# A two-layer hybrid backbone on one core: the place of two transposes and of one low part in the first layer's norms

## The chip, the cores and the metric

The kernel runs on one core of a Trainium2 chip. The metric is the device time of one execution in microseconds (us), lower is better; a figure for a kernel is the median of its runs.

## The reference

Two layers over 512 latent and 256 context tokens of width 1024, in float32. What matters here is where the norms stand:

```python
for layer in range(DEPTH):                    # DEPTH = 2
    y_l, y_c = mixer(modulate(x, sh1, sc1), modulate(ctx, csh1, csc1), w_in[layer], ...)
    x = post_norm(x, g1 * y_l, ln1_w, ln1_b)  # layer_norm(ALPHA * x + g1 * y_l) * w + b
    x = post_norm(x, g2 * swiglu(modulate(x, sh2, sc2), w_gate_up, w_down), ln2_w, ln2_b)
    # in the first layer the same for ctx
# modulate(x, shift, scale) = layer_norm(x) * (1 + scale) + shift
```

So after the mixer's output projection every token goes through a post-norm with weight and bias, and then through a second, plain norm with a modulation, before the next weight product can read it. The same stands after the feed-forward part, where the next product is the next layer's input projection.

## The kernel before

The 768 tokens lie as six tiles of 128 tokens (`tiles`; the first layer uses all six, `nt = 6`). A weight product keeps float32 accuracy by splitting both operands into a high and a low part of a reduced format: one product (`product`, lines 822 to 824) is three matmuls. GpSimd splits the weights as they come (line 736 the high part, line 739 the low one) into a ring of eight slots, and TensorE frees a slot by raising `ring_used` in its work on the last tile. For the activations ScalarE writes the high part (`high`, line 1626, into `act_hi`) and VectorE the low part (`low_part`, line 2122, into `act_lo`). Each engine has its own program with the order of its work written out; semaphores join them.

The last pass of a projection ahead of a norm (`last_pass`) goes tile by tile, eight products each (index `j`, 0 to 7). As soon as a tile's sum is complete, the norm of that tile begins on the other engines, so that the norms run beside the products of the later tiles. For the tile with number n in a norm the steps are:

- VectorE takes the sum out of PSUM (lines 2131 and 2133 or 2135), makes statistics (2150, 2153), and applies the post-norm in `affine` (2204, 2206, 2211; the last one also sums the row). Lines 2204 and 2211 are the long steps, of 128x1024 elements.
- ScalarE takes the square root for the first norm (1589), then squares for the second norm (1596, `sd2`, which waits for line 2211) and takes its root (1599).
- VectorE turns it into a scale (`second_scale`, 2217 and 2218).
- ScalarE writes the normed tile to `xn` (1607, `normalize`).
- TensorE transposes it, eight 128x128 pieces into PSUM banks 6 and 7 (`transposes`, 918).
- ScalarE modulates it into `hbuf` (1613; for the last two tiles VectorE does half of it, 2183) and writes the high part (1626), and VectorE the low part (2122).

VectorE's and ScalarE's loops (`norm_steps` in each program) are skewed by steps. In VectorE's, step s has, in this order: `affine(s - 1)`, `low_part(s - 3)`, `modulate_half(s - 2)` (which does something for the last two tiles alone), the sum and statistics of tile s, `second_scale(s - 1)`. In ScalarE's, step s has `normalize(s - 2)`, `sd2(s - 1)`, `modulate(s - 2)`, the first root of tile s, `high(s - 2)`.

TensorE's transposes stand at fixed places in its own order. Tiles 0, 1 and 2 are transposed within the last pass, in its fourth, fifth and sixth tile, behind the product `j` that `NORM_SPOT` gives for that norm. A key is (layer, norm): (0, 1) is the first layer's norm after the mixer, (0, 2) the one after the feed-forward. Tiles 3, 4 and 5 are transposed in the work that follows. After norm (0, 1) that is the first gate-and-up chunks (`part` in `gate_up`): six parts of 48 matmuls with 256 columns, two chunks for each pair of tiles, the first chunk with weights in buffers of their own (`own_hi`, `own_lo`), the second from the ring. The transposes of tiles 3, 4 and 5 stand behind the first three parts, and the third and the fifth part wait for the low part of the pair's second tile (`wait_low`). After norm (0, 2) it is the next layer's input projection, eight products per tile, and transposes of tiles 3, 4 and 5 stand behind its first three tiles.

GpSimd splits the second gate-and-up unit as ring slots come free, and waits before the third for the low part of tile 4 (`wait_low(pool, ...)`). The norm (1, 1) (`MID`) has an order and places for its transposes of its own.

Of the kernel before, what the change touches and what calls it, by code (L numbers as in the profile page):

```python
# [41 lines left out]
SEGMENTS = {"win": [4] * 9, "modB": [0] * 8, "modG": [0] * 4, "wout": [4] * 4,  # L42
            "gu0": [4] * HALF, "dn0": [4, 4, 3, 3, 4, 4], "gu1": [4] * HALF, "dn1": [4, 4, 3, 4, 4, 3]}
KEPT = (3, 8)
NORM_SPOT = {(0, 1): (4, 5, 7), (0, 2): (3, 5, 6), (1, 1): (1,)}
MOD_BLOCKS = {"modA": [0, 1, 2, 3], "modB": [6, 7, 8, 9], "modG": [4, 5], "modC": [10, 11]}
START_TILES = [2, 3, 0, 4, 1, 5]

# [96 lines left out]
def build(nc, x, c, ctx_in, c_ctx, w_mod, b_mod, w_in, a_q_norm, a_k_norm, b_sink, f_mix, r_decay,  # L145
# [3 lines left out]
    with stack:  # L149
# [409 lines left out]
        def low_count(key, n):  # L559

            return n + 1 + (n + 1) // 2 if key == MID else n + 1
# [42 lines left out]
        def need(e, name, l, n):  # L604

            before = NORMS[:NORMS.index(l)] if isinstance(l, tuple) else range(l)
            e.wait_ge(sem(name), n + sum(signals(name, k) for k in before))
# [211 lines left out]
        def _(pe):  # L819
# [89 lines left out]
            def transposes(key, n):  # L909

                need(pe, "xn_ready", key, n + 1)
                if n > 0:
                    need(pe, "h_ready", key, n)
                    if shared_modulation(key, n - 1):
                        nt = len(tiles_of(key[0]))
                        need(pe, "h_half", key, signals("h_half", key) - (nt - n))
                for k in range(KC):
                    mm = nc.tensor.transpose(ps[:, 6 + k // 4, (k % 4) * P:(k % 4 + 1) * P], xn[:, n % 2, k * P:(k + 1) * P],  # L918
                                             ident[:, :])
                mm.then_inc(sem("xn_T"), 1)  # L920
# [445 lines left out]
            def last_pass(l, key, tiles, seg, p, g, m, left, ready):  # L1366

                nt = len(tiles)
                for n, t in enumerate(tiles):
# [3 lines left out]
                    for j in range(8):  # L1373
# [23 lines left out]
                        if key == MID:  # L1397
                            if (n, j) in ((2, 5), (3, 7)):
                                transposes(key, n - 2)
                        elif n >= 3 and key != (DEPTH - 1, 2) and j == NORM_SPOT[key][n - 3]:  # L1400
                            transposes(key, n - 3)
# [700 lines left out]
        def _(dve):  # L2102
# [3 lines left out]
            def link(ins):  # L2106

                step_no[0] += 1
                ins.then_inc(sem("dve_step"), 1)
                dve.wait_ge(sem("dve_step"), step_no[0])  # L2110
# [3 lines left out]
            def done(ins, name):  # L2114

                raised[name] = raised.get(name, 0) + 1
                ins.then_inc(sem(name), 1)
                dve.wait_ge(sem(name), raised[name])

            def low(dst, src, high):  # L2120

                return v.tensor_tensor(dst, src, high.bitcast(F32), ALU.subtract)
# [15 lines left out]
            def tail_part(h):  # L2138

                if h == 0:  # L2140
                    need(dve, "dn_acc", DEPTH - 1, 4 * (len(LAT) - 1) + 1)
                else:
                    dve.wait_ge(ring_used, dn_slot(DEPTH - 1, 3, HALF - 1) + 1)
                cols = slice(512 + h * 256, 768 + h * 256)
                link(v.tensor_tensor(tail_acc(h), tail_acc(h), bc[:, 0, cols], ALU.mult))  # L2145
                link(v.tensor_tensor(X[:, TAIL, cols], X[:, TAIL, cols], tail_acc(h), ALU.add))  # L2146
                link(v.bn_stats(st[:, TAIL, 6 + 6 * h:12 + 6 * h], X[:, TAIL, cols]))  # L2147

            def half_stats(t, o, h):
                return v.bn_stats(st[:, t, o + 6 * h:o + 6 * h + 6], X[:, t, h * 512:(h + 1) * 512])  # L2150

            def variance(t, o, signal):
                done(v.bn_aggr(st[:, t, o + 12:o + 14], st[:, t, o:o + 12]), signal)

            def norm_steps(key, tiles, first):
# [6 lines left out]
                def low_part(n):  # L2162
                    if not last and 0 <= n < len(tiles):
                        need(dve, "h_hi", key, low_count(key, n))
                        c = slice(tiles[n] * P, (tiles[n] + 1) * P)
                        done(low(act_lo[:, :, c], hbuf[:, n % 2, :].rearrange("p (k t) -> p k t", k=KC), act_hi[:, :, c]), "low_ready")
# [8 lines left out]
                def modulate_half(n):  # L2175
                    if last or not 0 <= n < len(tiles) or not shared_modulation(key, n):
                        return
                    need(dve, "xn_T", key, n + 1)
                    if n >= 2:
                        wait_low(dve, key, n - 2)  # L2180
                    stream = 0 if tiles[n] >= CT else 1
                    for k in range(4):
                        ins = v.tensor_scalar(hbuf[:, n % 2, k * P:(k + 1) * P], ps[:, 6, k * P:(k + 1) * P],  # L2183
                                              mod_col[:, 2 * which + 1, k, stream:stream + 1],
                                              mod_col[:, 2 * which, k, stream:stream + 1], ALU.mult, ALU.add)
                    done(ins, "h_half")

                def affine(n):
                    t = tiles[n]
                    if last and t == TAIL:  # L2190
                        halves = [slice(h * 512, (h + 1) * 512) for h in range(2)]
                        for c in halves:
                            ins = v.scalar_tensor_tensor(X[:, t, c], X[:, t, c], st[:, t, 18:19], bc[:, 2, c],  # L2193
                                                         ALU.subtract, ALU.mult)
                        link(ins)
                        need(dve, "sd1", key, n + 1)
                        link(v.reciprocal(st[:, t, 21:22], st[:, t, 20:21]))
                        for c in halves:
                            v.scalar_tensor_tensor(X[:, t, c], X[:, t, c], st[:, t, 21:22], bc[:, 3, c],  # L2199
                                                   ALU.mult, ALU.add).then_inc(sem("x_ready"), 1)  # L2200
                        return
                    if n == 0:
                        need(dve, "norm_in", key[0], 32 * key[1])
                    link(v.scalar_tensor_tensor(X[:, t, :], X[:, t, :], st[:, t, 12:13], bc[:, 2, :], ALU.subtract, ALU.mult))  # L2204
                    need(dve, "sd1", key, n + 1)
                    link(v.reciprocal(st[:, t, 15:16], st[:, t, 14:15]))
                    if last:
                        done(v.scalar_tensor_tensor(X[:, t, :], X[:, t, :], st[:, t, 15:16], bc[:, 3, :],  # L2208
                                                    ALU.mult, ALU.add), "x_ready")
                        return  # L2210
                    done(v.scalar_tensor_tensor(X[:, t, :], X[:, t, :], st[:, t, 15:16], bc[:, 3, :],
                                                ALU.mult, ALU.add, accum_out=st[:, t, 17:18]), "sum2")

                def second_scale(n):
                    t = tiles[n]
                    need(dve, "sd2", key, n + 1)
                    link(v.reciprocal(st[:, t, 32:33], st[:, t, 31:32]))
                    done(v.scalar_tensor_tensor(st[:, t, 33:34], st[:, t, 17:18], -1.0 / D, st[:, t, 32:33],
                                                ALU.mult, ALU.mult), "scale2")

                nt = len(tiles)
# [6 lines left out]
                if key == MID:  # L2228
# [23 lines left out]
                    low_half(3, 1)  # L2252
                    return
                for step in range(nt + 3):
                    if 0 < step <= nt:
                        affine(step - 1)
                    low_part(step - 3)
                    modulate_half(step - 2)
                    if last and step == nt - 1:
                        for h in range(2):  # L2260
                            tail_part(h)
                        done(v.bn_aggr(st[:, TAIL, 18:20], st[:, TAIL, 0:18]), "var1")
                    elif step < nt:
                        first(step, tiles[step])
                        link(half_stats(tiles[step], 0, 1))
                        variance(tiles[step], 0, "var1")
                    if 0 < step <= nt and not last:
                        second_scale(step - 1)
# [421 lines left out]
            for l in range(DEPTH):  # L2690
                tiles = tiles_of(l)
                nt = len(tiles)
# [53 lines left out]
```

## Time and profile before

| what | value |
| --- | --- |
| median of 3 runs | 1644.21 us (1642.68 to 1645.06) |
| profiled execution | 1643.62 us |
| its span, first to last instruction | 1641.8 us |
| TensorE matmuls busy | 1593.6 us, 97% |
| GpSimd busy | 855.9 us, 52% |
| VectorE busy | 778.2 us, 47% |
| ScalarE busy | 427.9 us, 26% |
| granted TensorE clock, mean | 0.998 of full speed |

The busy shares are means over stages of different kinds. The two norms of the change are short stages, 380 to 434 us and 950 to 1000 us, in which VectorE and ScalarE are nearly as busy as TensorE. Times in the rows are counted from the span's start. Matmuls are pipelined: a row's duration overlaps the next row's, so the pace of TensorE is read from the starts.

### The profile page before, as it was taken

The numbers are of one execution on the slowest core, as the hardware profiler recorded it, in microseconds if no ns is written. First come the engines' busy times: TensorE is split into PE (matmuls) and PEld (weight loads), VectorE is DVE, ScalarE is ACT, GpSimd is POOL, SyncE is SP. The second block draws the span as 40 slices with busy tenths as digits, with TensorE's granted clock in tenths as the row PEclk, the third lists the DMA queues.
The fourth block names the chain that finished last, engine by engine and source line by source line (L and its number), as shares of the span: only waits on it lengthen the run. The fifth ranks groups of instructions, "written<-read, shape, count | busy, mean of one in ns | idle before, by whom it ended". The sixth has DMA issues, their size and how long they took to land. (4 is left out here: it accounts for less than half of the span.)

```text
span 1641.8 us, 23300 instructions
## 1 busy us (share of the span) xinstructions
PE 1593.6 (97%) x9341; PEld 1359.3 (83%) x9341; DVE 778.2 (47%) x1200; ACT 427.9 (26%) x919; POOL 855.9 (52%) x850
## 2 busy tenths in 40 slices
PE   7999999999999999999999999999999999999997
PEld 5788766778999988899999888876777888888886
DVE  4462265549663414544554396715658322420038
ACT  5512365425400011100002064216534200200011
POOL 4643133643564444544445546613484777777772
PEclk9999999999999999999999999999999999999999
DMA  9312143121353312243652122210032642233321
GB/s 344 113 52 78 47 141 118 54 80 52 118 165 91 116 39 77 82 137 116 194 191 79 46 77 69 78 34 9 15 89 69 188 145 75 93 102 103 103 90 52
DMA packets 161369, 160.89 MB, mean 98 GB/s; under 512 B 6520, under 2 KB 120296, under 8 KB 161264
## 3 DMA queue, kind: packets, MB, share of 16 engines
q1 hardware_dynamic: 140928, 121.40, 24.4%
q10 hardware_dynamic: 20336, 38.03, 7.1%
q8 instruction: 74, 1.21, 0.3%
q14 instruction: 31, 0.25, 0.1%
HBM read 157.31 MB, written 2.10 MB: 97 GB/s over the span
## 5 line engine op out<-in xcount | busy, mean ns | idle before, releaser
L736 POOL TENSOR_SCALAR ring_hi<-stage 128x512 fp32r<-128x512 f32 x352 | 247.1, 702 | 523.9 <-PE ps L824 446.4
L739 POOL TENSOR_TENSOR ring_lo<-stage,ring_hi 128x512 fp32r<-128x512 f32 x352 | 480.6, 1365 | 29.4
L822 PE MATMUL ps<-act_hi,ring_hi 128*128 128x384 f32 (+2 forms) x1088 | 379.4, 349 | 2.1 <-POOL ring_lo L739 2.1
L824 PE MATMUL ps<-act_hi,ring_lo 128*128 128x384 f32 (+2 forms) x1088 | 377.8, 347 | 0.0
L823 PE MATMUL ps<-act_lo,ring_hi 128*128 128x384 f32 (+2 forms) x1088 | 377.8, 347 | 0.0
L822 PE MATMUL ps<-ring_hi,act_hi 128*128 128x512 f32 (+1 forms) x711 | 280.7, 395 | 1.9 <-ACT gate_ret L1755 1.5
L824 PE MATMUL ps<-ring_hi,act_lo 128*128 128x512 f32 (+1 forms) x711 | 273.5, 385 | 0.0
L823 PE MATMUL ps<-ring_lo,act_hi 128*128 128x512 f32 (+1 forms) x711 | 273.1, 384 | 0.0
L822 PEld LDWEIGHTS ps<-act_hi,ring_hi 128*128 128x128 f32 x1088 | 204.6, 188 | 15.9 <-POOL ring_lo L739 2.7
L823 PEld LDWEIGHTS ps<-act_lo,ring_hi 128*128 128x128 f32 x1088 | 204.6, 188 | 13.1
L824 PEld LDWEIGHTS ps<-act_hi,ring_lo 128*128 128x128 f32 x1088 | 204.5, 188 | 13.1
L2592 DVE TENSOR_TENSOR hid<-silu_g,ps 128x768 f32<-128x768 f32 (+1 forms) x44 | 36.1, 821 | 302.5 <-ACT silu_g L1981 302.2
L1981 ACT ACTIVATE silu_g<-ps 128x768 f32<-128x768 f32 (+1 forms) x44 | 31.0, 706 | 556.8 <-PE ps L824 526.8
L822 PEld LDWEIGHTS ps<-ring_hi,act_hi 128*128 128x128 f32 x711 | 133.7, 188 | 33.3 <-issue 6.4
L824 PEld LDWEIGHTS ps<-ring_hi,act_lo 128*128 128x128 f32 x711 | 133.6, 188 | 27.2
L823 PEld LDWEIGHTS ps<-ring_lo,act_hi 128*128 128x128 f32 x711 | 133.8, 188 | 26.2 <-issue 1.4
L749 POOL TENSOR_SCALAR probs<-probs,rden 128x768 f32<-128x768 f32 (+3 forms) x50 | 38.0, 767 | 133.7 <-DVE rden L2394 133.7
L2407 DVE SCALAR_TENSOR_TENSOR mod_acc_ffn<-mod_stage,c_silu,mod_acc_ffn 128x512 f32<-128x512 f32 x84 | 78.9, 966 | 16.7 <-DMA mod_stage<-in_w_mod_dram 14.9
L822 PE MATMUL ps<-ring_hi,hs_hi 128*128 128x512 f32 x220 | 86.6, 394 | 0.1
L824 PE MATMUL ps<-ring_hi,hs_lo 128*128 128x512 f32 x220 | 85.6, 389 | 0.0
L823 PE MATMUL ps<-ring_lo,hs_hi 128*128 128x512 f32 x220 | 85.6, 389 | 0.0
L2386 DVE TENSOR_REDUCE negmax<-ps 128x1 f32<-128x768 f32 (+4 forms) x80 | 57.8, 763 | 56.7 <-PE ps L1057 36.9
(278 smaller groups left out, 2040.2 us busy)
## 6 DMA issues: line engine op xcount, KB each, us to landing
stage<-in_w_gate_up_dram SPq DMA_DIRECT2D x88, 512.0 KB, 5.1
mod_stage<-in_w_mod_dram ACTq DMA_DIRECT2D x56, 512.0 KB, 4.1
stage<-in_w_in_dram SPq DMA_DIRECT2D x18, 1024.0 KB, 5.0
stage<-in_w_down_dram SPq DMA_DIRECT2D x16, 1024.0 KB, 5.0
stage<-in_w_mod_dram SPq DMA_DIRECT2D x12, 1024.0 KB, 5.2
start_mod<-in_w_mod_dram SPq DMA_DIRECT2D x16, 512.0 KB, 9.7
stage<-in_w_down_dram SPq DMA_DIRECT2D x8, 768.0 KB, 4.4
stage<-in_w_out_dram SPq DMA_DIRECT2D x16, 256.0 KB, 4.5
```

What stands on the lines that cost most here:

```text
L736: nc.gpsimd.tensor_scalar(hi_, stage[:, par, j * 512:(j + 1) * 512], 1.0, 0.0, ALU.mult, ALU.add).then_inc(w_hi, 1)
L739: nc.gpsimd.tensor_tensor(lo_, stage[:, par, j * 512:(j + 1) * 512], hi_.bitcast(F32), ALU.subtract).then_inc(w_ready, 1)
L749: nc.gpsimd.tensor_scalar(probs_slot(2 * i + a)[:, 0:n], probs_slot(2 * i + a)[:, 0:n], rden[:, m:m + 1], 0.0, ALU.mult, ALU.add).then_inc ...
L822: nc.tensor.matmul(o, a_hi, b_hi, start=first, stop=False)
L823: nc.tensor.matmul(o, a_hi, b_lo, start=False, stop=False)
L824: return nc.tensor.matmul(o, a_lo, b_hi, start=False, stop=last)
L1981: ins = a.activation(silu_g[:, e, lo_col:TOK].rearrange("p (r n) -> p r n", r=parts if fh or f > 1 else len(tiles_of(l)) // 2), gate_acc(l ...
L2386: v.tensor_reduce(negmax[:, m:m + 1], flat[:, 0:n], AX, ALU.max, negate=True).then_inc(sem("neg_ready"), 1)
L2407: return v.scalar_tensor_tensor(acc, w, c_k, acc, ALU.mult, ALU.add)
L2592: done(v.tensor_tensor(hid[:, j, lo_col:TOK].rearrange("p (r n) -> p r n", **pat), silu_g[:, e, lo_col:TOK].rearrange("p (r n) -> p r n", ...
```

## The change

Three edits. In norm (0, 1) the transposes of tile 1 stand behind product 7 of the fifth tile in place of product 5. In norm (0, 2) they stand behind product 6 in place of 5. In norm (0, 1), in VectorE's step 6 (`step == nt`), the low part of tile 3 stands ahead of `affine(5)` in place of behind it. The entry for (1, 1) is dropped from the table.

```diff
--- before.py
+++ after.py
@@ -42,7 +42,7 @@
 SEGMENTS = {"win": [4] * 9, "modB": [0] * 8, "modG": [0] * 4, "wout": [4] * 4,
             "gu0": [4] * HALF, "dn0": [4, 4, 3, 3, 4, 4], "gu1": [4] * HALF, "dn1": [4, 4, 3, 4, 4, 3]}
 KEPT = (3, 8)
-NORM_SPOT = {(0, 1): (4, 5, 7), (0, 2): (3, 5, 6), (1, 1): (1,)}
+NORM_SPOT = {(0, 1): (4, 7, 7), (0, 2): (3, 6, 6)}
 MOD_BLOCKS = {"modA": [0, 1, 2, 3], "modB": [6, 7, 8, 9], "modG": [4, 5], "modC": [10, 11]}
 START_TILES = [2, 3, 0, 4, 1, 5]
 
@@ -2252,9 +2252,12 @@
                     low_half(3, 1)
                     return
                 for step in range(nt + 3):
+                    if step == nt and key == (0, 1):
+                        low_part(step - 3)
                     if 0 < step <= nt:
                         affine(step - 1)
-                    low_part(step - 3)
+                    if step != nt or key != (0, 1):
+                        low_part(step - 3)
                     modulate_half(step - 2)
                     if last and step == nt - 1:
                         for h in range(2):
```

## Rows read from the trace of the kernel before

**Rows 1.** Stretches: us; busy us of PE, PEld, DVE, ACT, POOL; clock; DMA share, GB/s

```profile
434.00:959.00 525.00, 525.00 (x2857) 494.20 (x2856) 246.06 (x275) 51.41 (x66) 266.49 (x255) 1.00 0.37 114
```

**Rows 2.** Timeline of TensorE, first norm: start, duration, instruction, idle before and its releaser

```profile
396.85 0.39 PE L823 MATMUL ps<-ring_lo,act_hi 128*128 128x512 f32 x1
397.07 0.39 PE L824 MATMUL ps<-ring_hi,act_lo 128*128 128x512 f32 x1
398.29 1.09 PE L918 MATMUL ps<-ident_r,xn 128*128 128x128 f32 x8 [0.83 <-ACT xn L1607]
399.14 0.48 PE L822 MATMUL ps<-ring_hi,act_hi 128*128 128x512 f32 x1
...
420.01 1.09 PE L918 MATMUL ps<-ident_r,xn 128*128 128x128 f32 x8
421.90 0.39 PE L822 MATMUL ps<-act_hi,own_hi 128*128 128x256 f32 x1 [0.79 <-DVE act_lo L2122]
...
427.76 1.03 PE L918 MATMUL ps<-ident_r,xn 128*128 128x128 f32 x8
428.55 0.36 PE L822 MATMUL ps<-act_hi,ring_hi 128*128 128x256 f32 x1
```

**Rows 3.** Timeline of ScalarE, first norm

```profile
413.34 1.15 ACT L1596 ACTIVATE xn<-resid,st 128x1024 f32<-128x1024 f32 x1 [1.05 <-DVE resid L2211]
...
417.75 1.09 ACT L1626 ACTIVATE act_hi<-hbuf 128x1024 fp32r<-128x1024 f32 x1
418.70 1.26 ACT L1607 ACTIVATE xn<-resid,st 128x1024 f32<-128x1024 f32 x1
420.62 1.15 ACT L1596 ACTIVATE xn<-resid,st 128x1024 f32<-128x1024 f32 x1 [0.66 <-DVE resid L2211]
...
424.58 1.23 ACT L1607 ACTIVATE xn<-resid,st 128x1024 f32<-128x1024 f32 x1
```

**Rows 4.** Timeline of VectorE, first norm

```profile
403.46 1.28 DVE L2211 SCALAR_TENSOR_TENSOR resid<-resid,st,bc 128x1024 f32<-128x1024 f32 x1
404.78 1.51 DVE L2122 TENSOR_TENSOR act_lo<-hbuf,act_hi 128x1024 fp32r<-128x1024 f32 x1
...
409.02 0.40 DVE L2218 SCALAR_TENSOR_TENSOR st<-st 128x1 f32<-128x1 f32 x1
409.45 1.60 DVE L2204 SCALAR_TENSOR_TENSOR resid<-resid,st,bc 128x1024 f32<-128x1024 f32 x1
...
411.29 2.01 DVE L2211 SCALAR_TENSOR_TENSOR resid<-resid,st,bc 128x1024 f32<-128x1024 f32 x1
...
417.77 1.29 DVE L2204 SCALAR_TENSOR_TENSOR resid<-resid,st,bc 128x1024 f32<-128x1024 f32 x1
...
420.62 1.22 DVE L2122 TENSOR_TENSOR act_lo<-hbuf,act_hi 128x1024 fp32r<-128x1024 f32 x1
```

**Rows 5.** Timeline of GpSimd, first norm

```profile
404.34 0.88 POOL L736 TENSOR_SCALAR ring_hi<-stage 128x512 fp32r<-128x512 f32 x1 [23.66 <-PE ps L824]
405.31 2.12 POOL L739 TENSOR_TENSOR ring_lo<-stage,ring_hi 128x512 fp32r<-128x512 f32 x1
...
408.10 1.30 POOL L739 TENSOR_TENSOR ring_lo<-stage,ring_hi 128x512 fp32r<-128x512 f32 x1
...
410.07 2.15 POOL L739 TENSOR_TENSOR ring_lo<-stage,ring_hi 128x512 fp32r<-128x512 f32 x1
...
426.15 0.62 POOL L736 TENSOR_SCALAR ring_hi<-stage 128x512 fp32r<-128x512 f32 x1 [10.15 <-issue]
```

**Rows 6.** Timelines of TensorE and ScalarE, second norm

```profile
967.58 1.09 PE L918 MATMUL ps<-ident_r,xn 128*128 128x128 f32 x8 [0.66 <-ACT xn L1607]
...
988.03 1.05 PE L918 MATMUL ps<-ident_r,xn 128*128 128x128 f32 x8
...
981.07 1.15 ACT L1596 ACTIVATE xn<-resid,st 128x1024 f32<-128x1024 f32 x1 [0.15 <-DVE resid L2211]
...
986.67 1.26 ACT L1607 ACTIVATE xn<-resid,st 128x1024 f32<-128x1024 f32 x1
```

## The prediction

> **What bounds the kernel now.** I read the page's engine table first: TensorE is the engine that is hardly ever idle, so time is won or lost where it stands still, or where it is held for other engines. The table of stretches then says where not to look: from 434 to 959 us TensorE is busy 525.00 of 525.00 us [rows 1]. What it is late by at 434 it is late by at 959. Both places that the change touches are at the two ends of that stretch: the first layer's first norm (380 to 434 us) and its second (950 to 1000 us). Call the six transposes of a norm T0 to T5, one per tile in order of work.
>
> In the first norm the timeline of TensorE shows two stalls [rows 2]. Before T1 it issued matmuls at 396.85 and 397.07, could have gone on at 397.30, and started T1 at 398.29, released by ScalarE's xn: 0.99 us lost. Before the part for the third and fourth tiles it waited for VectorE's low part, at 421.90. The timelines of ScalarE [rows 3], VectorE [rows 4] and GpSimd [rows 5] show what stands behind them: ScalarE's and VectorE's steps are written out in one order, so an instruction that waits holds everything behind it.
>
> **T1 two products later, first norm.** A product is three matmuls; six matmuls at this pace of just under 0.23 us are 1.36 us, so T1 is reached at 398.66, after xn (398.25). No wait is left. A T that waited cost 0.85 us to the next matmul (398.29 to 399.14), one that didn't 0.79 (427.76 to 428.55) [rows 2]. So TensorE is ahead by 0.99 + 0.06 = 1.05 us. How far? T4 started at 420.01, 0.05 after ScalarE's xn for it (418.70 + 1.26 = 419.96) [rows 2, 3]. ScalarE's xn is fed from VectorE: its square pass started at 413.34, as VectorE's long step from 411.29 for 2.01 us ended [rows 3, 4]. Nothing in this chain waits for T1. T4 therefore doesn't move, and by itself the 1.05 us is worth 0 at T4.
>
> But one thing does start earlier: GpSimd. Its first split started at 404.34 when TensorE's work on the last tile had freed a ring slot [rows 5]. Now that is at 403.29. At 403.46 VectorE starts an affine step of 1.28 us (L2211) [rows 4]. Before, VectorE was first, and GpSimd's split took 0.88 instead of 0.62. Rows where GpSimd was first: the low part at 404.78 took 1.51 instead of 1.22 (GpSimd's L736 ended 405.22); L2211 at 411.29 took 2.01 instead of 1.28 (L739 from 410.07 ended 412.22); the small step at 409.02 took 0.40 and ended with L739, at 409.40 [rows 4, 5]. The other way, L739 at 405.31 took 2.12 instead of 1.30 and ended 1.14 after the low part's end at 406.29. So whoever comes second waits for the first's end. In the sum I use these distances: a long VectorE step ends 1.07 after GpSimd's end, L739 1.15 after VectorE's end, L736 0.48 after.
>
> Replayed with GpSimd at 403.29: L736 ends 403.91. VectorE's L2211 (403.46) is held, +0.30, ends 405.04. L739 ends 406.19. The low part (405.08) is held by it, ends 407.26: +0.96. L736 ends 407.74, L739 409.12, L736 409.71; the next L739 starts 409.78 and ends 411.08, just ahead of VectorE's small step, now at 409.99: +0.95. L2204 at 411.13 is held by the last L736 (ends 411.67): +0.33. L2211 at 412.98 is held by the last L739 (ends 413.89): +0.70, ends 414.96. That is 3.24 us of holding where before there were 0.29 + 0.24 + 0.31 + 0.73 = 1.57: VectorE's step for the fifth tile ends 1.67 us later. Ends for this term: 0 if GpSimd comes after 403.46 (0.17 us of margin decides, and then the pattern of before repeats); 0.6 if the small step at 409.99 slips ahead of L739 (margin 0.21); 1.8 if all are held longest. I take 1.67, nearest to the rows.
>
> The Trainium skill, page "SBUF — State Buffer", section "Who interferes with whom", states this as a rule: VectorE instructions with two SBUF inputs and GpSimd instructions that read SBUF take a shared port as an exclusive lock, and whoever issues first holds it for its whole length. The trace agrees, with the pairs above. By a rule of shared bandwidth both would be slowed in proportion, whatever the order, and the term would be near 0.
>
> **The fourth tile's low part first, first norm.** Before: affine(5) at 417.77, the low part at 420.62, 1.22 us [rows 4]. The low part needs ScalarE's high part, from 417.75 [rows 3], done 418.84 (1.09 long). With about 0.1 for the hand-over (estimate; ScalarE to TensorE took 0.05 above) it runs from 418.95 to 420.17. TensorE's wait at 421.90 is gone: T4 at 420.01 plus 0.85 lets it go on at 420.86, so 1.04 us is won here. Ends for it: 0 and 1.04.
>
> What is queued behind the waiting low part is affine(5): from 420.20 instead of 417.77, +2.43. ScalarE's square pass for the last tile (420.62) waits for that, and behind it stand, in ScalarE's order, the fifth tile's modulation and high part and the last tile's xn at 424.58 [rows 3]. All go 2.43 later. That xn was done at 425.81, and T5 at 427.76 didn't wait: 1.95 us of cover [rows 2, 3]. Now it is done at 428.24, T5 starts 428.29 and the next matmul 429.14 instead of 428.55: +0.59, where TensorE alone would have been 1.04 early. So the won wait comes back, larger, at T5. GpSimd's unit at 426.15 [rows 5] waits for the fifth low part and moves by as much, but TensorE asks for its slots only after two more parts of 5.8 us, and no wait follows.
>
> Both parts together: the 1.67 shifts the whole chain from 413.34 on. xn of T4 comes at 421.63 (TensorE is there a good 2 us before), and T5's next matmul at 429.14 + 1.67 = 430.81 against 428.55: **+2.26 us** at 434, kept to 959. VectorE's own steps between (low part of the third tile ends 416.2) are done before the later high part, so they add nothing. The last low part still has about a us before the third pair's part asks for it.
>
> **T1 one product later, second norm.** T1 waits there, at 967.58 [rows 6], by 0.82 (0.66 idle, plus the tail of the matmul before); one product is 0.68, so it still waits 0.14, starts when it did, and the 0.68 is taken out behind it. Again T4 bounds it: TensorE reached it at 988.03, while xn was ready at 987.93. ScalarE needed 5.60 us from square pass to xn (981.07 to 986.67), in the first norm for the same steps 5.36 (413.34 to 418.70), since T3 held it a little [rows 3, 6]. That 0.24 goes; with it T4 comes at 987.74, 0.29 earlier, and costs 0.06 more as one that waits: **-0.23 us**. Ends: 0 and -0.68. GpSimd stands still in this stage. The dropped table entry (1, 1) is read by nobody: that norm's spots stand in code of their own. No DMA is moved in its queue; stage loads only follow GpSimd.
>
> **Sum.** +2.26 - 0.23 = +2.03 us on the profiled execution's 1643.62 (span 1641.8 and 1.8 around it) is 1645.65. It stands 0.59 below the median of the runs, 1644.21; on that, 1646.2.
>
> **The rivals.**
> *No collision (25%).* GpSimd's earlier start doesn't hold VectorE more than before. For it: 0.17 us decides, and GpSimd's records are the roughest. Against: a short lead was enough before (L2204 at 409.45 took 1.60, held by a split that can't have started until the L739 of 408.10 was over, at 409.40). Then +0.59 - 0.23 = +0.36: 1644.6.
> *The cover at T5 holds (17%): the faster side.* Place: ScalarE's queue between the low part and T5. If the low part doesn't wait for its high part, or ScalarE runs the last tile's steps sooner than in-order, xn comes no later than 426.76, where TensorE reaches T5 (421.90 to 427.76 is 5.86; 420.86 + 5.86 = 426.72). The point is a delay of 0.9 us: below it all of 1.04 stays. Then -1.04 - 0.23 = -1.27: 1642.9. Against: the high part ends only at 418.84, so a delay under 1.2 us would need it 1.2 earlier.
> *Long stalls cost clock (6%).* The waits at T4 and T5 are now some 2.4 and 1.6 us within 10. The granted clock is 1.00 in the row of stretches [rows 1], the 2.4 GHz level. If it fell to 1.2 GHz for a part, that part of 5.86 us would take as long again: 1652.
> *Nothing measurable by either (4%)*: 1644.2. The forecast has 48%.
>
> What a measurement of this kernel can tell from no change is about 0.2%, 3.3 us. Every case but the clock lies within it, so the sign is more a matter of the trace than of the times. Faster by over 0.2%: 2%; within: 90%; slower: 8%. The range runs from the case of the faster side to somewhat over the forecast, for the spread of the runs (1642.68 to 1645.06): 1643.0 to 1647.6. The forecast's own is 1645.0 to 1647.4.
>
> **What the next profile would show.** Right: T1 at 398.7 with no wait; GpSimd's first split at 403.3 with 0.62; L2211 at 403.46 near 1.6 and the low part behind it over 2 us; T4 near 421.7 and T5 near 430.0, both waiting for ScalarE's xn; no wait of TensorE for the fourth low part; 434 to 959 still full. Wrong: T4 at 420.0 (no collision), or T5 at 426.7 (the cover held). In the second norm T4 waits near 987.7.

## The result, and the profile after

The changed kernel takes 1646.41 us (median of 21 runs, 1644.41 to 1650.17), the kernel before 1643.96 in the same comparison (21 runs, 1642.40 to 1648.21): ratio 1.0015, 95% interval 1.0009 to 1.0021. It is slower by 2.4 us, 0.15%. The profiled execution took 1645.79 us, its span is 1644.0.

Single executions reach the first norm up to a few us earlier or later. T0, the first of a norm's six transposes, stands at 390.28 before and at 388.94 after, ahead of anything that was changed. So positions are compared from T0 on: 1.34 is to be added to a time of after. First TensorE's timeline in the first norm, the answer to [rows 2]; columns as there.

```profile
388.94 1.03 PE L918 MATMUL ps<-ident_r,xn 128*128 128x128 f32 x8
...
397.34 1.03 PE L918 MATMUL ps<-ident_r,xn 128*128 128x128 f32 x8
...
405.91 0.39 PE L822 MATMUL ps<-act_hi,own_hi 128*128 128x256 f32 x1 [1.19 <-DVE act_lo L2122]
...
420.27 1.09 PE L918 MATMUL ps<-ident_r,xn 128*128 128x128 f32 x8 [1.71 <-ACT xn L1607]
421.12 0.36 PE L822 MATMUL ps<-act_hi,own_hi 128*128 128x256 f32 x1
...
428.55 1.09 PE L918 MATMUL ps<-ident_r,xn 128*128 128x128 f32 x8 [1.43 <-ACT xn L1607]
429.40 0.36 PE L822 MATMUL ps<-act_hi,ring_hi 128*128 128x256 f32 x1
```

T1 (397.34) waits no more, and neither does the part behind T4 (421.12). In their place stand three other waits: 1.19 us ahead of the part behind T2, for VectorE's low part, and 1.71 and 1.43 us at T4 and T5, for ScalarE's xn. From T0 to the matmul behind T5 it is 40.46 us, before 38.27 (428.55 less 390.28 [rows 2]): 2.19 us longer. VectorE and GpSimd show where it begins, the answers to [rows 4] and [rows 5]:

```profile
402.14 1.50 DVE L2211 SCALAR_TENSOR_TENSOR resid<-resid,st,bc 128x1024 f32<-128x1024 f32 x1
...
403.68 2.17 DVE L2122 TENSOR_TENSOR act_lo<-hbuf,act_hi 128x1024 fp32r<-128x1024 f32 x1
...
408.58 1.11 DVE L2218 SCALAR_TENSOR_TENSOR st<-st 128x1 f32<-128x1 f32 x1
409.73 1.61 DVE L2204 SCALAR_TENSOR_TENSOR resid<-resid,st,bc 128x1024 f32<-128x1024 f32 x1
...
411.57 1.99 DVE L2211 SCALAR_TENSOR_TENSOR resid<-resid,st,bc 128x1024 f32<-128x1024 f32 x1
...
419.20 1.23 DVE L2122 TENSOR_TENSOR act_lo<-hbuf,act_hi 128x1024 fp32r<-128x1024 f32 x1 [1.48 <-ACT act_hi L1626]
420.46 1.28 DVE L2204 SCALAR_TENSOR_TENSOR resid<-resid,st,bc 128x1024 f32<-128x1024 f32 x1
```

```profile
401.95 0.62 POOL L736 TENSOR_SCALAR ring_hi<-stage 128x512 fp32r<-128x512 f32 x1 [22.62 <-PE ps L824]
402.65 2.12 POOL L739 TENSOR_TENSOR ring_lo<-stage,ring_hi 128x512 fp32r<-128x512 f32 x1
...
408.38 1.30 POOL L739 TENSOR_TENSOR ring_lo<-stage,ring_hi 128x512 fp32r<-128x512 f32 x1
```

GpSimd's first split (401.95) now leads VectorE's L2211 (402.14) by 0.19 us. L2211 takes 1.50, the low part behind it 2.17. The small step L2218 starts at 408.58, 0.20 behind an L739, and takes 1.11 us for one element per partition; both end together, at 409.68 and 409.69. The low part at 419.20 stands ahead of the last affine, which starts at 420.46. ScalarE's timeline shows what that holds up, the answer to [rows 3]:

```profile
413.60 1.15 ACT L1596 ACTIVATE xn<-resid,st 128x1024 f32<-128x1024 f32 x1 [2.63 <-DVE resid L2211]
...
423.31 1.15 ACT L1596 ACTIVATE xn<-resid,st 128x1024 f32<-128x1024 f32 x1 [3.09 <-DVE resid L2211]
...
427.27 1.23 ACT L1607 ACTIVATE xn<-resid,st 128x1024 f32<-128x1024 f32 x1
```

The square pass of the fifth tile (413.60) is 1.60 us later counted from T0, that of the last tile (423.31) 4.03, and the last xn, done at 428.50, is what T5 at 428.55 waits for. Between the norms nothing changes, as in [rows 1]; the columns are as there.

```profile
434.00:959.00 525.00, 525.00 (x2861) 494.34 (x2860) 244.36 (x273) 51.70 (x67) 268.10 (x258) 1.00 0.37 114
```

In the second norm T4 now waits for the xn that starts at 987.24 (TensorE and ScalarE, the answer to [rows 6]):

```profile
968.38 1.09 PE L918 MATMUL ps<-ident_r,xn 128*128 128x128 f32 x8
...
988.55 1.09 PE L918 MATMUL ps<-ident_r,xn 128*128 128x128 f32 x8
```

```profile
987.24 1.26 ACT L1607 ACTIVATE xn<-resid,st 128x1024 f32<-128x1024 f32 x1
```

The norm's T0 to T5 are 35.10 us, before 35.32. From the first norm's T0 to the end of the span the profiled execution of after is 3.5 us longer. The edits' share of it is 1.9, and nearly all the rest lies in the next layer's norm (1, 1), which the change doesn't touch: there the granted clock was at 0.50 for 3.4 us, right after two waits of 0.92 and 0.97 us, and the matmuls followed each other at 0.21 us in place of 0.12. Before, the same two waits stood there and the clock stayed at 1.00. From one transpose to the next there (1270.17 to 1279.26 after, 1269.52 to 1277.11 before) that is 1.50 us. The row of the stretch, and matmuls at its beginning:

```profile
1275.70:1279.10 3.40, 3.40 (x17) 3.40 (x17) 1.02 (x1) 1.04 (x1) 0.00 (x0) 0.50 0.75 219
```

```profile
1275.49 0.45 PE L822 MATMUL ps<-act_hi,ring_hi 128*128 128x256 f32 x1 [0.97 <-POOL ring_lo L739]
...
1275.96 0.42 PE L824 MATMUL ps<-act_hi,ring_lo 128*128 128x256 f32 x1
1276.17 0.42 PE L822 MATMUL ps<-act_hi,ring_hi 128*128 128x256 f32 x1
```

### The profile page after: what moved, and what is told of

Read it like the earlier page. It is cut to its first block and busy times, and to the rows that moved or that the text cites. A ratio compares the mean times of both kernels' runs of the same rounds, so it can differ in the third digit from the quotient of the medians.

```text
span 1644.0 us, 23300 instructions
## 1 busy us (share of the span) xinstructions
PE 1594.5 (97%) x9341; PEld 1360.5 (83%) x9341; DVE 778.1 (47%) x1200; ACT 428.2 (26%) x919; POOL 854.4 (52%) x850
## 5 line engine op out<-in xcount | busy, mean ns | idle before, releaser
L739 POOL TENSOR_TENSOR ring_lo<-stage,ring_hi 128x512 fp32r<-128x512 f32 x352 | 479.3, 1362 | 29.4
```

Source lines behind the costliest of these rows:

```text
L739: nc.gpsimd.tensor_tensor(lo_, stage[:, par, j * 512:(j + 1) * 512], hi_.bitcast(F32), ALU.subtract).then_inc(w_ready, 1)
```

## The experiments

The expectations name a "port collision": the prediction's account that of a VectorE and a GpSimd instruction the one that comes second waits for the other's end. They were written after the changed kernel's trace was known, so they test which edit costs what, and in experiments 4 and 5 the order of arrival, more than the size of a hold.

All are read in two ways: by the median against runs of the kernel before on the same chip, and by stretches of one profiled execution. A is from T0 of the first norm to T0 of the second, B from T0 to T5 of the second; the unchanged kernel gives both again within 0.05 us, and the two runs of experiment 4 differ by 0.10 in A. Clock is the mean of the granted clock over the timed runs; for the kernel before it is taken over its 93 runs beside the experiments.

| kernel | A, us | B, us | median, us | before | ratio, 95% interval | clock |
| --- | --- | --- | --- | --- | --- | --- |
| before | 568.79 | 35.32 | | | | 0.9977 |
| the change | 570.92 | 35.10 | 1646.41 | 1643.96 | 1.0015, 1.0009 to 1.0021 | 0.9973 |
| unchanged | 568.75 | 35.31 | 1642.68 | 1643.40 | 0.9997, 0.9988 to 1.0006 | 0.9979 |
| 1: first norm's T1 | 570.15 | 35.32 | 1646.55 | 1643.88 | 1.0015, 1.0007 to 1.0024 | 0.9965 |
| 2: low part | 569.34 | 35.30 | 1644.61 | 1643.88 | 1.0002, 0.9993 to 1.0011 | 0.9974 |
| 3: second norm's T1 | 568.76 | 35.09 | 1645.52 | 1643.88 | 1.0006, 0.9997 to 1.0015 | 0.9969 |
| 3 again | 568.75 | 35.11 | 1643.65 | 1643.69 | 0.9999, 0.9990 to 1.0008 | 0.9979 |
| 4: change, GpSimd later | 569.35 | 35.11 | 1646.92 | 1643.88 | 1.0014, 1.0005 to 1.0023 | 0.9965 |
| 4 again | 569.45 | 35.06 | 1644.89 | 1643.69 | 1.0011, 1.0002 to 1.0019 | 0.9973 |
| 5: GpSimd later alone | 569.21 | 35.35 | 1644.71 | 1643.40 | one run | |
| 6: low part between, with 3 | 568.16 | 35.09 | 1643.66 | 1643.40 | 1.0003, 0.9994 to 1.0012 | 0.9975 |
| 6 without 3 | 568.17 | 35.33 | 1643.25 | 1643.69 | 0.9998, 0.9989 to 1.0006 | 0.9975 |
| 7: and T5 inside, with 3 | 567.69 | 35.09 | 1644.09 | 1643.40 | 1.0005, 0.9995 to 1.0015 | 0.9971 |
| 7 without 3 | 567.69 | 35.33 | 1642.78 | 1643.69 | 0.9995, 0.9986 to 1.0004 | 0.9972 |

**1. The first norm's T1 alone.**

```diff
-NORM_SPOT = {(0, 1): (4, 5, 7), (0, 2): (3, 5, 6), (1, 1): (1,)}
+NORM_SPOT = {(0, 1): (4, 7, 7), (0, 2): (3, 5, 6), (1, 1): (1,)}
```

> Only the first norm's transposes of the second tile two products later (first layer, norm after the mixer). Measured from T0 to the matmul behind T5 (38.27 us before, 40.46 after the whole change). My theory (port collision, 1.60 us on VectorE's step for the fifth tile): GpSimd's first split starts ahead of VectorE's L2211 for the fourth tile, the small step L2218 takes 1.1 us, T4 starts some 1.3 to 1.6 us later, and the stretch is 39.6 us, +1.35; the kernel is about 1.3 us slower. Rival 1 (only VectorE's new order costs; the later T1 is a plain gain or nothing): the stretch is 37.2 to 38.3. Rival 2 (the loss is the clock's, not this stage's): the stretch is 38.3, and the times scatter with the granted clock.

T0 to the matmul behind T5: 39.60 us (389.56 to 429.16), against the 39.6 of the port collision. Moving T1 off its wait alone makes the stage 1.33 us longer. VectorE's small step has the length of the changed kernel, and T4 and the part behind it wait; VectorE's row, then TensorE's:

```profile
409.20 1.12 DVE L2218 SCALAR_TENSOR_TENSOR st<-st 128x1 f32<-128x1 f32 x1
```

```profile
420.90 1.09 PE L918 MATMUL ps<-ident_r,xn 128*128 128x128 f32 x8 [1.72 <-ACT xn L1607]
422.50 0.39 PE L822 MATMUL ps<-act_hi,own_hi 128*128 128x256 f32 x1 [0.51 <-DVE act_lo L2122]
```

**2. The low part alone** (the change's edit of VectorE's loop, all transposes as before).

> Only the fourth tile's low part ahead of the last affine step; all transposes where they were. My theory: GpSimd and VectorE meet as before (L2218 0.40, L2211 2.01), the wait for the low part goes, ScalarE's square pass for the last tile comes 2.4 us later and T5 waits for xn: from T0 to the matmul behind T5 38.27 + 0.59 = 38.86 us; the kernel is 0.6 us slower. Rival 1 (the order is the gain, the cover at T5 holds): 37.2 us. Rival 3 (all 2.2 us come from the order): 40.4 us.

38.87 us (390.51 to 429.38) against an expected 38.86: 0.60 longer than before. The rows of VectorE, ScalarE and TensorE: the small step is as before, the last square pass waits 3.08 us (0.66 before), and T5 waits.

```profile
409.28 0.39 DVE L2218 SCALAR_TENSOR_TENSOR st<-st 128x1 f32<-128x1 f32 x1
```

```profile
423.29 1.15 ACT L1596 ACTIVATE xn<-resid,st 128x1024 f32<-128x1024 f32 x1 [3.08 <-DVE resid L2211]
```

```profile
428.53 1.09 PE L918 MATMUL ps<-ident_r,xn 128*128 128x128 f32 x8 [1.43 <-ACT xn L1607]
```

**3. The second norm's T1 alone, run twice.**

```diff
-NORM_SPOT = {(0, 1): (4, 5, 7), (0, 2): (3, 5, 6), (1, 1): (1,)}
+NORM_SPOT = {(0, 1): (4, 5, 7), (0, 2): (3, 6, 6), (1, 1): (1,)}
```

> Only the second norm's transposes of the second tile one product later. My theory: T0 to T5 of that norm 35.32 - 0.22 = 35.10 us, T4 waits for xn, the first norm's stretch stays 38.27; the kernel is 0.2 us faster, which the times can't show. Rival: 0.68 us, the whole product, is won: 34.64.

> The kernel with the second norm's T1 one product later alone, once more. Stretch 35.10 us. If its excess over before in the median (1.6 us where the stretch gives -0.2) belongs to the kernel, it comes again with a mean clock below 0.9975; if it was the clock's own scatter, the median is now within 0.7 us of before.

B is 35.09 and 35.11: 0.2 us won, not 0.68. The median was 1.6 above before the first time and level with it the second, with the mean clock 0.9969 and 0.9979. So the excess did not come again.

**4. The whole change, with GpSimd's first split one ring slot later, run twice.**

```diff
-pool.wait_ge(ring_used, g0 - (15 if seg == "gu0" and i == 2 else 7))
+pool.wait_ge(ring_used, g0 - (15 if seg == "gu0" and i == 2 else 6 if (l, seg, i, j) == (0, "gu0", 1, 0) else 7))
```

> The whole change, but GpSimd's first split of the second gate-and-up unit waits for one more ring slot (six products of the last tile in place of five, 0.68 us later), so that VectorE's L2211 is first again. My theory: L2211 takes 1.28, L2218 0.40, the long steps are held as before the change, and the stretch from T0 to the matmul behind T5 is 38.86 us, the same as with the low part's move alone; the kernel is 0.4 us slower than before and 1.6 faster than the changed one. Rival 1 and 3 (no collision: the order alone costs): 40.4 us, as the changed kernel, or longer by the later start.

> The whole change with GpSimd's first split one ring slot later, once more. Stretches 38.88 and 35.10 us. By the stretches its median is 0.4 us above before and 1.6 below the changed kernel; the first time it was 3.0 above before. If that excess belongs to the kernel it comes again, with a mean clock near 0.9965; if it was scatter, it goes.

T0 to the matmul behind T5 is 38.89 and 38.85 us: a start of GpSimd 0.68 us later takes 1.6 us off the stage, and with T1 moved it is as long as with the low part's move alone. The 1.6 us are the collision's price, and with it gone the wait taken from T1 is seen to have been worth nothing. VectorE's and GpSimd's rows: GpSimd (405.65) now comes behind L2211 (405.17), which takes 1.28, and the small step takes 0.40.

```profile
405.17 1.28 DVE L2211 SCALAR_TENSOR_TENSOR resid<-resid,st,bc 128x1024 f32<-128x1024 f32 x1
...
410.74 0.40 DVE L2218 SCALAR_TENSOR_TENSOR st<-st 128x1 f32<-128x1 f32 x1
```

```profile
405.65 1.28 POOL L736 TENSOR_SCALAR ring_hi<-stage 128x512 fp32r<-128x512 f32 x1 [23.30 <-PE ps L824]
```

The medians did not follow: 3.0 and 1.2 above before, where the stretches give 0.35 and 0.40. The excess shrank the second time but stayed. Both profiled executions had stretches of low clock besides the one at the very end that every execution has, two and three of them, where that of the kernel before had none.

The low clock is not all of it. Behind the second norm, where the next layer's mixer begins, the first trace of this kernel has a second collision that came out the other way. VectorE, GpSimd and TensorE, in experiment 4 and then in the kernel before:

```profile
1026.52 2.20 DVE L2303 TENSOR_TENSOR tmp<-tmp,rope_grid 128x192 f32<-128x192 f32 x2
1026.49 0.62 POOL L736 TENSOR_SCALAR ring_hi<-stage 128x512 fp32r<-128x512 f32 x1 [1.65 <-PE ps L824]
1036.36 0.90 PE L945 MATMUL ps<-ident_r,post 128*128 128x128 f32 x3 [2.30 <-DVE post L2309]
```

```profile
1024.41 1.04 DVE L2300 TENSOR_TENSOR tmp<-tmp,rope_grid 128x192 f32<-128x192 f32 x2
1024.45 0.80 POOL L736 TENSOR_SCALAR ring_hi<-stage 128x512 fp32r<-128x512 f32 x1 [1.70 <-PE ps L824]
1032.95 0.55 PE L945 MATMUL ps<-ident_r,post 128*128 128x128 f32 x3 [1.06 <-DVE post L2306]
```

Before, VectorE was 0.04 us ahead of GpSimd; here GpSimd was 0.03 ahead, VectorE's two steps took 2.20 in place of 1.04, and TensorE stood 2.30 us in place of 1.06. From the second norm's T5 to this transpose it is 39.92 us, before 38.56: 1.36 us lost, with the clock at 1.00 until 0.18 us before the wait ended (the low stretch begins at 1036.18). The low stretch behind it cost the other 1.5. The second trace of the same kernel kept the order of before.

**5. The kernel before, with GpSimd one ring slot later** (the edit of 4 alone).

> The kernel before, with GpSimd's first split of the second unit 0.68 us later and nothing else. My theory (whoever comes second waits for the other's end): VectorE's low part at 404.8 takes 1.22, not 1.51, but its small step L2218 now comes just behind an L739 and takes 1.1 in place of 0.40; VectorE's step for the fifth tile ends 0.4 us later, and so do T4 and the low part: T0 to the matmul behind T5 38.7 us. Rival (a shared port slows both by a share, or GpSimd later only relieves VectorE): 38.0 to 38.3.

38.69 us (389.20 to 427.89), as the port collision had it; the rival's 38.0 to 38.3 is out. A GpSimd that comes later relieves the low part (1.23) and still makes the stage 0.4 us longer, since the small step now falls behind an L739. VectorE's row, then GpSimd's:

```profile
407.67 1.11 DVE L2218 SCALAR_TENSOR_TENSOR st<-st 128x1 f32<-128x1 f32 x1
```

```profile
407.47 1.29 POOL L739 TENSOR_TENSOR ring_lo<-stage,ring_hi 128x512 fp32r<-128x512 f32 x1
```

**6. The fourth low part between the two long steps of the last affine, with and without 3.**

```diff
                     link(v.reciprocal(st[:, t, 15:16], st[:, t, 14:15]))
+                    if key == (0, 1) and n == len(tiles) - 1:
+                        low_part(n - 2)
...
-                    low_part(step - 3)
+                    if step != nt or key != (0, 1):
+                        low_part(step - 3)
```

> The first norm's T1 where it was before; the fourth tile's low part between the two long steps of the last affine (behind L2206, ahead of L2211) in place of ahead of both; the second norm's T1 one product later as in the change. My theory: the low part then waits for nothing (its high part ends 418.84, L2206 ends 419.25), the last L2211 comes 1.25 us later, the cover at T5 (1.95 less the 1.04 won) takes 0.9 of it: T0 to the matmul behind T5 is 37.7 us, 0.6 less than before; second norm T0 to T5 35.10; together 0.8 us faster than before. If a low part put forward costs ScalarE's queue its full wait wherever it stands, 38.9.

> The low part between the long steps and nothing else. T0 to the matmul behind T5 37.7 us, second norm 35.32: 0.6 faster than before; the median as that of before less 0.6, within the scatter of the clock.

37.69 and 37.70 us, 0.6 less than before: the order gains once the low part no longer waits for its high part. VectorE, ScalarE, TensorE: no idle before the low part, 1.92 us before the square pass in place of experiment 2's 3.08, and T5 waits 0.26.

```profile
420.17 1.23 DVE L2122 TENSOR_TENSOR act_lo<-hbuf,act_hi 128x1024 fp32r<-128x1024 f32 x1
```

```profile
422.75 1.15 ACT L1596 ACTIVATE xn<-resid,st 128x1024 f32<-128x1024 f32 x1 [1.92 <-DVE resid L2213]
```

```profile
427.99 1.09 PE L918 MATMUL ps<-ident_r,xn 128*128 128x128 f32 x8 [0.26 <-ACT xn L1607]
```

**7. As 6, and T5 inside the following part, with and without 3.**

```diff
                             if (l, f, r, gu, j) == (DEPTH - 1, 1, 0, 1, 1):
                                 transposes((l, 1), 3)
+                            if (l, f, r, gu, j) == (0, 1, 1, 0, 0):
+                                transposes((l, 1), 5)
...
-                        if rest and (key != MID or len(rest) == 2):
+                        if rest and (len(rest) == 2 if key == MID else len(rest) > 1):
```

> As the kernel with the low part between the long steps, and T5 of the first norm stands 0.72 us later, inside the following part behind its first ring slot, so that TensorE doesn't wait for xn. My theory: all of the 1.04 us is kept, the last low part (ends near 432.8) still comes before TensorE asks at 433.4; from T0 to the second norm's T0 568.79 - 1.04 = 567.75 us; with the second norm 1.3 us faster than before. Rival: TensorE waits for the last low part instead, and the stretch is 568.2.

> The kernel with the low part between the long steps and T5 inside the following part, with the second norm as it was before the change. Stretches by my theory: T0 to the second norm's T0 567.7 us (568.8 before), second norm 35.32: 1.04 faster than before. If the moved T1 of the second norm goes with more stretches of the low clock (the kernel with that alone: mean clock 0.9969, before 0.9978), this kernel's mean clock is as before and its median 1 us below; if the clock scatters by itself, its median lies within 1 us either way.

A is 567.69 in both, 1.1 us less than before, all of what the low part's wait had cost. T5 waits for nothing:

```profile
426.24 1.04 PE L918 MATMUL ps<-ident_r,xn 128*128 128x128 f32 x8
```

By the stretches, 7 with 3 is the best version, 1.3 us below the kernel before and 3.2 below the changed one. Its median doesn't show that against before (0.7 above), and that of 7 without 3 is 0.9 below with an interval that holds 1. Against the changed kernel both are lower (1644.09 and 1642.78 to 1646.41, measured beside other runs of before).

**The unchanged kernel.**

> The kernel before, unchanged, as a kernel of its own: what the comparison shows of no change. Stretches 38.28, 530.5 and 35.32 us as before; median within 0.5 us of the kernel before. If its times lie 1 to 2 us above, the differences in the medians that the stretches don't show (second norm alone: +1.6 us for -0.2) are the comparison's own.

It comes out 0.7 us below itself: at least that much a median of 11 runs can be off.

## Why the prediction was right

Forecast +2.03 us, measured +2.45 in the medians, 1646.2 to 1646.41; the stretches from T0 of the first norm to T5 of the second give 2.13 - 0.22 = +1.91. The median of 21 runs can't tell these apart, and its closeness to the forecast is partly luck: over the experiments, medians lay from 0.7 below to 2.7 above what the stretches give. So it is for the profiled execution, 1645.79 against 1645.65: its way to T0 was 1.34 us shorter than before's, and its low stretch cost 1.50. What carries the verdict is the stretches, term by term.

- *T1 moved in the first norm, worth 0 at T4.* Held: T4 starts 0.05 after ScalarE's xn in both kernels, and experiment 4 against 2 gives 0.
- *The collision, 1.67 us.* Measured 1.60 at the fifth tile's square pass. GpSimd led L2211 by 0.19 (0.17 forecast), L2211 was held 0.22 (0.30), the low part 0.95 (0.96), the small step 0.95 (0.95), L2204 0.32 (0.33), L2211 0.71 (0.70). The first was a slip of the working: it ended 1.07 after GpSimd's split, the distance that the prediction had stated, which makes 0.24, not the 0.30 that was put in, and 1.61 in all. The order hung on margins of 0.17 and 0.21 us; they came out as 0.19 and 0.20, in experiment 1's trace too. Experiments 1, 4 and 5 confirm it from three sides, the last with the order of arrival turned round. The rule of the Trainium skill, "SBUF — State Buffer", "Who interferes with whom", stands here by these numbers: issue order decides, and the second waits for the first to end, but for its first 0.2 us or so (a step that alone takes 1.28 us ended 1.07 after GpSimd's split).
- *The low part first: 1.04 won at T4, the wait back at T5, +0.59 in all.* Experiment 2 measured +0.60, and so refutes the rival of the cover that holds.
- *Second norm, -0.23.* Measured -0.22.
- *Not foreseen:* the part behind T2 waits 1.19 us for the second tile's low part, which the replay had ending (407.26) 1.4 us after TensorE could start there (405.85). The number was in the working and its reader wasn't looked for. It cost nothing, since T4 holds TensorE later by more. But it took up the 1.05 us by which TensorE was ahead: the last matmul ahead of T4 started at 418.28, which is 419.62 by before's count, and before it started at 419.63. So the wait at T4 was 1.71 us, not the 2.4 that the prediction had.
- *Long stalls cost clock.* The profiled executions show no low clock in or behind the first norm's two new waits of 1.7 and 1.4 us. Stretches of it stand in other places, near 28, 216, 1036 and from 1262 to 1286 us, in some executions and not in others.

What stays open is why some medians lie above their stretches. The low mean clocks go with high medians, and the repeats of 3 and 4 came out lower than the first runs by 1.9 and 2.0 us. But it is not the clock alone. In the first run of experiment 4 the two fastest executions, 1644.45 and 1644.59 us, have a mean clock of 0.999, and the fastest of before beside them took 1642.38 with the same clock: 2.1 us, where the stretches give 0.35. The collision near 1026 us could be this: in experiment 4's first trace it costs 1.36 us. Its order hangs on a few hundredths of a us in all fourteen traces. With the second norm's T1 in its old place VectorE was first by 0.03 to 0.06; with it moved by 0.00 to 0.02 in six traces, and last in the seventh. And the median lay above the stretches by 0.2 to 2.7 us in all seven comparisons of kernels with that move, by -0.7 to 1.3 in the five without. No experiment took this collision apart, and with one trace for each kernel the frequency of either order, and of the low stretches, isn't known. So the small gain of the second norm's edit, 0.22 us in its stretch, may cost more further on; that is not shown.

The fastest run of each kernel against the fastest of before beside it follows the stretches better than the medians do: within 0.6 us for all but the first run of experiment 4.

## What to carry to other kernels

A wait taken off one engine is worth only what the next joint lets through: here the next transposes hung on an in-order chain of two other engines, and an engine that arrives early only starts something else early. Before moving a step ahead in an in-order queue, ask whether it will itself wait there, and who is queued behind: between the two long steps the same low part waited for nothing and gained 0.6 us, and 1.1 with T5 moved as well. Where VectorE and GpSimd both stream from SBUF, replay who comes first, small instructions too: a one-column step lost 0.95 us here. And follow a shift of some hundredths of a us to the next place where the two meet; a tie there can turn.

## What the runs showed of the hardware

GpSimd 1.05 us earlier made VectorE's chain 1.6 us longer, GpSimd 0.68 us later 0.4 us longer (experiments 1 and 5); the holds repeat within 0.02 us from run to run, so such a stage can be worked out where the order is clear by 0.2 us. The granted clock fell to 0.50, the 1.2 GHz level, for 3.4 or 6.8 us in some executions and not in others: behind the same two waits of 0.92 and 0.97 us it fell in after and stayed up in before. The stretches of 3.4 us in the norm (1, 1) and just behind it cost 1.4 to 1.6 us each. The way to T0 differs too, from 388.94 to 393.96 us over the fourteen traces. The runs of one kernel spread over 2.0 to 7.4 us, mostly more than any edit here moved, while the stretches repeat within 0.1.
